# State space products over all 128 rows: one input matrix for two channel groups, and tables with zeros for the states of two groups

## The reference, cut to what matters

```python
def s5_mixer(u, log_dt, a_re, a_im, b_re, b_im, c_re, c_im, d_skip, w_glu, b_glu):
    ...
    x_re = jnp.einsum('bsgc,gpc->sbgp', ug, bbar_re.astype(dtype))
    x_im = jnp.einsum('bsgc,gpc->sbgp', ug, bbar_im.astype(dtype))
    ...
    _, _, h_re, h_im = lax.associative_scan(_complex_affine_combine, elems, axis=0)
    y = (jnp.einsum('sbgp,gcp->bsgc', h_re, c_re)
         - jnp.einsum('sbgp,gcp->bsgc', h_im, c_im))
    y = y.reshape(bsz, seq, SSM_WIDTH) + d_skip * u
    g = jax.nn.gelu(y)
    return g * jax.nn.sigmoid(g @ w_glu + b_glu)
```

## Time and profile before

| what | us |
|---|---|
| median of 3 runs | 1262.01 |
| lowest and highest run | 1259.06, 1269.68 |
| the profiled execution, its own time | 1266.62 |
| its span in the trace | 1265.0 |
| TensorE busy | 1199.2 |
| VectorE, ScalarE, GpSimd busy | 818.4, 518.4, 429.8 |
| mean granted TensorE clock | 0.988 |

### The profile page before, as it was taken

One profiled execution on the slowest core, in us unless ns is written; L12 is line 12 of the kernel. 1 busy time (PEld: TensorE's weight loads), 2 busy tenths in 40 slices (PEclk: granted clock), 3 DMA queues, 4 the chain that ended last, 5 costly groups with the idle time before them and its releaser, 6 DMA issues.

```text
span 1265.0 us, 18760 instructions
## 1 busy us (share of the span) xinstructions
PE 1199.2 (95%) x6336; PEld 1017.2 (80%) x6336; DVE 818.4 (65%) x1379; ACT 518.4 (41%) x975; POOL 429.8 (34%) x392
## 2 busy tenths in 40 slices
PE   7999999988999998999999999997989999999996
PEld 6998888877888886888788888876868888888875
DVE  5625382267787776676677885845779758555684
ACT  6513211257777773344243332312223336443541
POOL 0089231154555530000815666655664400000000
PEclk9999999999999998999999999998989999999998
DMA  9233352296545522133224556454443239955641
GB/s 349 77 101 83 134 119 100 100 258 170 132 130 132 116 60 67 51 101 120 88 81 142 193 200 232 158 183 174 174 163 134 85 130 335 357 199 185 211 171 67
DMA packets 82391, 191.72 MB, mean 152 GB/s; under 512 B 21478, under 2 KB 21526, under 8 KB 81164
## 3 DMA queue, kind: packets, MB, share of 16 engines
q1 hardware_dynamic: 70220, 148.06, 33.9%
q0 software_dynamic: 11824, 42.04, 12.6%
q10 hardware_dynamic: 288, 0.85, 0.2%
HBM read 133.41 MB, written 56.91 MB: 150 GB/s over the span
## 4 chain that ended last, share of the span: by engine, by line
PE 70%; issue 7%; POOL 7%; DMA 6%; DVE 5%; ACT 3%; SPq 0%; POOLq 0%; DVEq 0%; ACTq 0%
PE ps L2315 7%; PE ps L2370 5%; PE ps L2371 5%; PE ps L2372 5%; PE ps L2389 5%; PE ps L2390 5%; PE ps L2391 5%; POOL op_f L1825 4%; PE ps L512 4%; PE ps L514 3%; PE ps L513 3%; DMA wd_scratch<-op_f 3%; PE ps L2224 3%; POOL s_sum L1825 3%; PE ps L2343 2%
## 5 line engine op out<-in xcount | busy, mean ns | idle before, releaser
L2370 PE MATMUL ps<-t_hi,s_hi 128*128 128x512 f32 x304 | 120.4, 396 | 13.8 <-DVE s_lo L1223 13.7
L2389 PE MATMUL ps<-dn_hi 128*128 128x512 f32 x308 | 120.2, 390 | 1.5 <-DVE dn_lo L1223 1.4
L2390 PE MATMUL ps<-dn_lo,dn_hi 128*128 128x512 f32 x308 | 119.9, 389 | 0.0
L2391 PE MATMUL ps<-dn_hi,dn_lo 128*128 128x512 f32 x308 | 119.8, 389 | 0.0
L2372 PE MATMUL ps<-t_hi,s_lo 128*128 128x512 f32 x304 | 119.7, 394 | 0.0
L2371 PE MATMUL ps<-t_lo,s_hi 128*128 128x512 f32 x304 | 119.7, 394 | 0.0
L1157 ACT ACTIVATE dn_hi<-rw 128x1024 fp32r<-128x1024 f32 x77 | 81.2, 1059 | 86.9 <-DMA rw<-wd_scratch 34.0
L1223 DVE TENSOR_TENSOR ev<-ps,ev 128x512 f32<-128x512 f32 x133 | 89.2, 682 | 33.2 <-PE ps L2372 33.0
L1223 DVE TENSOR_TENSOR dn_lo<-rw,dn_hi 128x1024 fp32r<-128x1024 f32 x77 | 91.9, 1220 | 26.0 <-ACT dn_hi L1157 25.0
L1223 DVE TENSOR_TENSOR s_lo<-s_sum,s_hi 128x512 fp32r<-128x512 f32 x72 | 62.6, 870 | 59.8 <-ACT s_hi L1122 59.7
L1223 DVE TENSOR_TENSOR ptl<-ps,pth 128x512 fp32r<-128x512 f32 (+1 forms) x120 | 76.2, 636 | 30.8 <-ACT pth L1016 28.4
(11 more groups left out here) (306 smaller groups left out, 3112.6 us busy)
## 6 DMA issues: line engine op xcount, KB each, us to landing
rw<-hid_scratch SPq DMA_DIRECT2D x77, 256.0 KB, 3.9
op_f<-w_down POOLq DMA_DIRECT2D x11, 1024.0 KB, 6.4
wd_scratch<-op_f POOLq DMA_DIRECT2D x11, 1024.0 KB, 4.7
rw<-wd_scratch SPq DMA_DIRECT2D x44, 256.0 KB, 4.8
hid_scratch<-ol_f SPq DMA_DIRECT2D x10, 1024.0 KB, 5.1
w_raw<-w_stream SPq DMA_DIRECT2D x18, 512.0 KB, 3.9
raw_b<-w_stream SPq DMA_DIRECT2D x18, 512.0 KB, 6.3
rw<-w_down SPq DMA_DIRECT2D x33, 256.0 KB, 4.3
```

The lines of the kernel that those rows point to most:

```text
L2370: pe.matmul(out, s_hi[:, j, k], x_hi[:, k, :], start=k == 0, stop=False)
L2389: pe.matmul(out, a_hi, b_hi, start=k == 0, stop=False)
L2390: pe.matmul(out, a_hi, b_lo, start=False, stop=False)
L2391: return pe.matmul(out, a_lo, b_hi, start=False, stop=k == KH - 1)
```

## The change

Two products are rearranged, and the tables they need are built on GpSimd.

- `kl` is formed for two groups at a time. A new table `b_pair` (in the space of `bc`) holds 32 columns for each pair: 16 with the rows of the even group and zeros below, 16 with zeros above and the rows of the odd group. Eight pairs take 2 products each, over all 128 rows, instead of 16 groups with 2 products over 64 rows. The result fills 32 rows of two banks, and ACT copies it twice instead of four times.
- For y all 128 rows of `hs` are used for each group. So the table must be zero in the rows of the other group: the odd groups' half is copied to `d_odd` (in the space of `mt`), whose even rows are zero, and the odd rows of `dre` and `dim` themselves are then set to zero.
- POOL builds `b_pair` ahead of its first `qk_low`, and `d_odd` between its `qk_low` of chunk 4 and of chunk 5, once DVE has read `mt` (a new copy on DVE behind the scans signals `z_read`). TensorE waits for `b_pair` ahead of `kl` and for `d_halves` ahead of the products with `hs`.
- Since `kl` now lies in 2 x 16 partitions, the Toeplitz matrix is built with 16 DMAs of half the size instead of eight.

```diff
-S5_PE = before(ut_mm=4, mb_mm=4, kl_mm=4, x_mm=1, y_mm=1, gt_mm=4, glu_mm=1)
+S5_PE = before(ut_mm=4, mb_mm=4, kl_mm=2, x_mm=1, y_mm=1, gt_mm=4, glu_mm=1)
...
+        b_pair = bc[:].rearrange("p (r q) j o -> p r (q j o)", r=2).rearrange("p r (j h o) -> p r j h o", j=NJ, h=2)
         kl = hs[:].rearrange("p r j c -> p (r j) c")
+        d_odd = mt
...
-            for a in range(4):
+            for a in range(2):
                 act.wait_ge(s5_pe, S5_PE["kl_mm"] + a + 1)
-                ins = act.activation(kl[0:CH, group_at(a, 0):group_at(a, 3) + 1:2, :],
-                                     ps[0:CH, 4 + a, :].rearrange("p (g c) -> p g c", g=4), ACT.Copy)
+                ins = act.activation(kl[0:2 * CH, 4 * a:4 * a + 4, :],
+                                     ps[0:2 * CH, 4 + a, :].rearrange("p (g c) -> p g c", g=4), ACT.Copy)
...
             link(ins)
+            dve.tensor_copy(q(TC), q(T1)).then_inc(s5_dve, 1)
             evacuate_qk(4, 2, 0)
             ahead(split_low, dve, 5, 2, 1)
 
-            dve.wait_ge(tz_in, 16 * TS)
+            dve.wait_ge(tz_in, 32 * TS)
...
+            link(pool.memset(bc[:], 0.0))
+            for h in range(2):
+                rows_ = slice(ST * h, ST * (h + 1))
+                ins = pool.tensor_copy(b_pair[rows_, :, :, h, :], bbar[rows_])
+                if h == 0:
+                    link(ins)
+            ins.then_inc(s5_pool, 1)
+            pool.wait_ge(s5_pool, S5_POOL["b_pair"] + 1)
...
             for s in range(TS):
-                pool.dma_start(tz[CH * s:CH * (s + 1), :, CH * s:P], kl[0:CH, :, 0:P - CH * s]).then_inc(tz_in, 16)
-
-            with pool.Fori(0, 3) as i:
+                for h in range(2):
+                    pool.dma_start(tz[CH * s:CH * (s + 1), h:G:2, CH * s:P],
+                                   kl[CH * h:CH * (h + 1), 0:NJ, 0:P - CH * s]).then_inc(tz_in, 16)
+
+            for j in range(2):
+                qk_low_parts(3 + j, 1 - j)
+
+            even, odd = slice(0, ST), slice(ST, P)
+            pool.wait_ge(s5_dve, S5_DVE["z_read"] + 1)
+            link(pool.memset(d_odd[even], 0.0))
+            for r, d in enumerate((dre, dim_)):
+                link(pool.tensor_copy(d_odd[odd, r], d[odd, :, 1:TS + 1, :].rearrange("p j l o -> p j (l o)")))
+                ins = pool.memset(d[odd], 0.0)
+                if r == 0:
+                    link(ins)
+            ins.then_inc(s5_pool, 1)
+            pool.wait_ge(s5_pool, S5_POOL["d_halves"] + 1)
+
+            with pool.Fori(1, 3) as i:
...
-            pe.wait_ge(s5_pool, S5_POOL["d_done"] + 1)
-            for a in range(4):
+            pe.wait_ge(s5_pool, S5_POOL["b_pair"] + 1)
+            for a in range(2):
                 for b in range(4):
-                    g = group_at(a, b)
-                    r, j = slice(ST * (g % 2), ST * (g % 2 + 1)), g // 2
-                    out = ps[0:CH, 4 + a, b * P:(b + 1) * P]
-                    pe.matmul(out, bbar[r, 0, j, :], dre[r, j, 0:TS, :], start=True, stop=False)
-                    last = pe.matmul(out, bbar[r, 1, j, :], dim_[r, j, 0:TS, :], start=False, stop=True)
+                    j = 4 * a + b
+                    out = ps[0:2 * CH, 4 + a, b * P:(b + 1) * P]
+                    pe.matmul(out, b_pair[:, 0, j], dre[:, j, 0:TS, :], start=True, stop=False)
+                    last = pe.matmul(out, b_pair[:, 1, j], dim_[:, j, 0:TS, :], start=False, stop=True)
                 last.then_inc(s5_pe, 1)
...
+            pe.wait_ge(s5_pool, S5_POOL["d_halves"] + 1)
             for half_ in range(2):
-                r = slice(ST * half_, ST * (half_ + 1))
                 for j in range(NJ):
                     out = y_out(2 * j + half_)
-                    pe.matmul(out, hs[r, 0, j, :], dre[r, j, 1:TS + 1, :], start=False, stop=False)
-                    last = pe.matmul(out, hs[r, 1, j, :], dim_[r, j, 1:TS + 1, :], start=False,
+                    d_re, d_im = ((d_odd[:, r, j, :] for r in range(2)) if half_ else
+                                  (d[:, j, 1:TS + 1, :] for d in (dre, dim_)))
+                    pe.matmul(out, hs[:, 0, j, :], d_re, start=False, stop=False)
+                    last = pe.matmul(out, hs[:, 1, j, :], d_im, start=False,
                                      stop=bank_of(2 * j + half_)[1] == 3)
```

More of the change, by code:

```diff
@@ L78, in before @@
     return out
-S5_PE = before(ut_mm=4, mb_mm=4, kl_mm=4, x_mm=1, y_mm=1, gt_mm=4, glu_mm=1)
+S5_PE = before(ut_mm=4, mb_mm=4, kl_mm=2, x_mm=1, y_mm=1, gt_mm=4, glu_mm=1)
 S5_ACT = before(ut_out=1, mb_out=1, kl_out=1, gelu_done=1, gt_out=1, glu_sig=1, y_ssm_sq=1)
-S5_DVE = before(mt_done=1, h_done=1, y_sum=1, glu_sum=1, y_gated=1)
-S5_POOL = before(d_done=1, e_done=1, tz_zero=1, du_done=1)
+S5_DVE = before(mt_done=1, z_read=1, h_done=1, y_sum=1, glu_sum=1, y_gated=1)
+S5_POOL = before(d_done=1, e_done=1, tz_zero=1, du_done=1, b_pair=1, d_halves=1)
 C_QK = 0
@@ L2157, in _ @@
             pe.wait_ge(s5_dve, S5_DVE["h_done"] + 1)
-            pe.wait_ge(tz_in, 16 * TS)
+            pe.wait_ge(tz_in, 32 * TS)
             def y_out(g):
```

## The result

| | median us | range | executions |
|---|---|---|---|
| before | 1257.82 | 1250.35 to 1269.68 | 20 |
| changed | 1251.09 | 1246.50 to 1257.77 | 20 |

What follows compares the result with a forecast made beforehand. TensorE's own queue was taken to bound the kernel; `kl` -3.1 us and y +0.3 us gave -2.8 us, so the median would go from 1262.0 to 1259.2 us, range 1254 to 1266.

Steps and rivals of the forecast that it cites:

- Rival D: In `kl`, new products with 32 columns need twice 109 ns, so only y's 0.3 us cost remains: 1262.3 us; chance 0.05.
- the other end I named: In y, all 96 records at 112 ns instead of 114.4: 10.72 us, 0.06 us more than before.
- The two covers: Margins before TensorE waits: 3.7 us for chunk 6 behind the `tz` DMAs, 2.8 to 4.0 for `w_lo` of chunk 7.
- Rivals A and B: TensorE waits before chunk 7: A, clearings hinder DVE, 1261.9 us, chance 0.12; B, slower copies too, about 1264.5, chance 0.05.
- the rule I weighed: On DVE beside POOL's `d_odd` work: two-SBUF-input operations contend only with GpSimd SBUF reads; copies hinder 2.2 us, clearings nothing.
- the sum: Whole-kernel gain: `kl` 3.1 us less plus y 0.3 us more, -2.8 us, with all behind chunk 7 moving along.
- Rival C: Elsewhere in the kernel, the shift moves a clock fall in TensorE's waits away: 3 us more gain, 1256 us; chance 0.08.

Runs made afterwards that it cites:

- the change run again: The unaltered changed kernel timed once more beside the kernel before: 1249.2 us, ratio 0.9918.
- the runs with shortened operations: POOL's four operations on each `w_down` block cut to 64 of 512 columns, in the kernel before (1247.8 us) and in the changed kernel (1246.6 us).
- the halves in turns: Kernel before with `kl` and y still over 64 rows, but products of even and odd groups alternating: 1252.5 us, ratio 0.9935.
- the loop written out: Kernel before with TensorE's loop over chunks 4 to 7 written out, no product changed: 1252.4 us, ratio 0.9946.
- y alone: Kernel before with only `d_odd` and the y products over 128 rows; `kl` and the eight `tz` DMAs as before: 1259.3 us, ratio 0.9984.
- changed + 64: Changed kernel with 64 semaphore increments added at the head of TensorE's queue: 1258.3 us, ratio 0.9962 against the kernel before.
- `kl` alone: Kernel before with only `kl` over 128 rows, `b_pair` and 16 `tz` DMAs; y as before, no `d_odd`: 1252.4 us, ratio 0.9944.
- by halves: `kl` as changed, y with alternating row halves, no `d_odd`, POOL loading and storing each `w_down` block in two halves: 1243.6 us, ratio 0.9862 against before.

## Why the prediction was wrong

What it said of the changed stages held:

- `kl`: 32 records at 109 to 110 ns (153.71 to 157.01 is 3.30 us for 30), 4.36 us in all against 4.33 forecast. Rival D (32 columns at twice the price) is out.
- y: forecast 0.3 us more, measured 0.03 less. The 128-row records go at 112 ns, the other end I named (for 64 of them 7.06 us, 7.00 before), and the 32 records of `tz` take 3.57 us (3.66).
- The two covers held. `tz` took 8.41 us (forecast 9.0), `qk_low` of chunk 3 ended at 169.15 (169.6), `d_odd` took 7.5 us with its gaps (6.1 to 8.7), and it was ready at 188.8 (190). DVE lost 1.5 us beside the copies (2.2) and none beside clearings; it also began its six operations at 177.91, before the 178.4 to 179.6 of the forecast. Rivals A and B are out, and the rule I weighed (SBUF — State Buffer, the lock of the shared port pair, in the Trainium skill) is borne out in both halves; the later copy is the longer one (1.92 against 1.41 us), so the wait goes both ways.

The step that failed is the last sentence of the sum: "Everything behind chunk 7 follows TensorE and moves with it." The events did move with it for 460 us, up to 731; then a chain off TensorE's queue, POOL's turned weights, set the time, and it did not move with it. My profile had the wait of 13.7 us for `s_lo` at the head of TensorE's waits, and a spread of 10 us among three executions; I took both for given. Of the 10 us between before and the change run again, 3.1 are gained ahead of attention, the term I worked out, and 7.0 behind it, where the runs with shortened operations show this chain.

The starting level was off too. The forecast of 1259.2 us was 2.8 off a median of 1262.0 from three executions; over 20 it is 1257.8. So of the 8.1 us between 1259.2 and the measured 1251.1, 4.2 are the level and 3.9 the part of the gain that the sum did not have.

Rival C forecast about 3 us more than the sum, and from its direction: a wait of TensorE that a shift moves out of the way. It was partly right in its cause as well. The mean clock barely differs (0.988 and 0.990), but in the feed-forward layer before has two falls of 6.8 us and the changed kernel none, as shown above; the changed execution has one of 3.4 us at 1209.7 instead and one of 6.8 us, not 3.4, at the start of attention. Over eleven profiled executions with the chain whole, the clock fell there in the six with a wait for `s_lo` of 4.3 us or more, and in none of the five whose longest was 1.5. So the falls follow the waits and add to them. Wrong in C is the trigger, which is not the shift but the length of TensorE's queue: the halves in turns shifted more and kept the late store, the loop written out shifted nothing and lost it.

Over the same eleven the two sets do not overlap in the wait on the store. The four with a fetch beside the store (before, y alone, in turns, changed + 64) waited 5.75 to 6.04 us for it, the seven without 4.50 to 4.52. The times agree: from attention's start to the end the medians are 984.4 to 987.1 us for the kernels with the fetch and 976.9 to 982.0 for those without. The waits for `s_lo` in a single execution do overlap (6.4 to 13.7 and 0 to 9.3 us), because later stores of the loop come late too (waits of 6.0 to 8.2 us from 777 us on, in kernels of both sets), and from 736 to 999 us no such fetch lies in any trace. What makes those late was not traced.

What also stays open is why `kl` alone (mean 1252.5) and the change (1250.1, run again) differ by 2.4 us, when both start the attention at 270.3 to 270.4 and neither has the fetch; with twelve executions each and standard deviations of 2.5 the difference is some two and a half times its standard error, and no run explains it.

## What to carry to other kernels

Before a local gain is carried through to the end, look in the rest of the trace for the longest waits of the bounding engine and for a chain of single-buffered loads and stores whose period is close to that engine's (here 19.8 against 19.0 us): such a chain has no slack, and what touches it, here the length of another engine's queue, can cost or give more than the edit. A wide spread between executions of the kernel before was a sign of it; then mend the chain first (here by halves, 1243.6 us) and measure small changes after. For products over half the rows, take the halves in turns before filling the other rows with zeros.

## What the runs showed of the hardware

- An instruction fetch is a DMA packet of 16 KB that lasted 0.93 us on one DMA engine; where one began as POOL issued a store of 1 MB, POOL waited 5.8 to 6.0 us for the landing instead of 4.5.
- The granted clock fell to half for 3.4 to 10.2 us in the feed-forward layer where TensorE had waited 4.3 to 8.7 us, and did not fall at waits of 1.0 to 1.5 us.
- Float32 products over alternate halves of the rows go at 56 ns a record, over one half or over all 128 rows at 109 to 114. The Trainium skill (TensorE: Matmul & The Clock Gate, Part 3: Packing small matmuls) says that products on different row groups run at once, and here that was worth 3.2 us in y (10.63 to 7.43).
- Semaphore increments in TensorE's queue took 0.15 us each (192 of them from 1.1 to 30.3 us), and the first product came 22.9 us later.
- A store of 512 KB from POOL landed in 3.2 us, one of 1 MB in 4.6 (medians). With each block in halves, the idle time for landings fell from 67.8 to 22.5 us.
